# Two attention stages and a recurrence stage of a two-layer mixer: fetches on ScalarE's queue, queries and keys written reordered, a third PSUM bank

## The reference, cut to what matters

```
p = softmax(s)                                   # differential attention, 4 heads, two maps each
a = p[:, :, 0] - lam * p[:, :, 1]
y_a = rms_norm(a @ v) * ... * silu(az)

# mLSTM: chunkwise recurrence in both directions over 768 tokens, 4 heads of 128
num = a_inter * (q @ C) + (qk * exp(...)) @ v

# neighbourhood attention on a grid of 8 rows x 64 columns, 8 heads of 64
s_loc = q @ k[rows, 32 columns] * scale + bias   # for each block of 16 query columns
s_ctx = q @ k_ctx * scale
y_c = softmax([s_loc, s_ctx]) @ [v_loc, v_ctx] * silu(cz)

x = x + gate * (sum_n sigmoid(gm_n) * (y_n @ w_br_n)) @ w_out
```

## Time and profile before

| | |
|---|---|
| median of 3 runs | 3079.73 us |
| the profiled execution, its own time | 3081.52 us |
| span of its instructions | 3079.7 us |
| TensorE busy | 2865.6 us, 93% |
| VectorE busy | 1917.6 us, 62% |
| ScalarE busy | 1383.1 us, 45% |
| mean granted TensorE clock | 0.981 |

### The profile page before, as it was taken

One profiled execution on the slowest core, in us unless ns is written; L12 is line 12 of the kernel. 1 busy time (PEld: TensorE's weight loads), 2 busy tenths in 40 slices (PEclk: granted clock), 3 DMA queues, 4 the chain that ended last, 5 costly groups with the idle time before them and its releaser, 6 DMA issues. The chain is left out here.

```text
span 3079.7 us, 49691 instructions
## 1 busy us (share of the span) xinstructions
PE 2865.6 (93%) x19876; PEld 1760.7 (57%) x19876; DVE 1917.6 (62%) x3554; ACT 1383.1 (45%) x2817; POOL 35.7 (1%) x108
## 2 busy tenths in 40 slices
PE   7997899899999898899899989999999989999998
PEld 3564656755565464656544555366655656666654
DVE  6437666677534747766675568677734458777734
ACT  3236654454432336555454453444423248744422
POOL 0000000000000000000000000000000001100000
PEclk8999999999999999999999999999999989999999
DMA  8422321155432323331464323223324420023322
GB/s 334 170 79 63 76 94 62 56 149 118 88 113 79 104 81 88 83 100 69 145 155 139 113 81 117 89 83 112 108 95 134 134 74 2 21 91 110 110 94 84
DMA packets 190185, 315.56 MB, mean 102 GB/s; under 512 B 138589, under 2 KB 144349, under 8 KB 169349
## 3 DMA queue, kind: packets, MB, share of 16 engines
q1 hardware_dynamic: 185301, 307.01, 31.6%
q10 hardware_dynamic: 4656, 5.38, 0.5%
HBM read 261.83 MB, written 6.34 MB: 87 GB/s over the span
## 5 line engine op out<-in xcount | busy, mean ns | idle before, releaser
L315 PE MATMUL banks<-h_sb,wsplit_sb 128*128 128x512 f16 (+2 forms) x6528 | 1219.0, 340 | 64.8 <-PEq L86 19.6
L315 PEld LDWEIGHTS banks<-h_sb,wsplit_sb 128*128 128x128 f16 x6528 | 627.1, 99 | 567.4 <-issue 96.3
L315 PE MATMUL banks<-quads,wsplit_sb 128*128 128x512 f16 (+2 forms) x3300 | 589.9, 337 | 4.6 <-PEq L86 4.6
L290 ACT ACTIVATE wsplit_sb<-ring_sb 128x1024 f16<-128x1024 f32 (+2 forms) x356 | 330.1, 943 | 416.8 <-PE banks L315 374.6
L300 DVE SCALAR_TENSOR_TENSOR wsplit_sb<-ring_sb,wsplit_sb 128x1024 f16<-128x1024 f32 (+2 forms) x356 | 381.9, 1088 | 217.4 <-ACT wsplit_sb L290 215.4
L315 PEld LDWEIGHTS banks<-quads,wsplit_sb 128*128 128x128 f16 x3300 | 320.7, 98 | 256.4 <-issue 10.6
L315 PE MATMUL banks<-wsplit_sb,h_sb 128*128 128x256 f16 x2112 | 242.8, 274 | 7.9 <-ACT quads L559 3.2
L315 PEld LDWEIGHTS banks<-wsplit_sb,h_sb 128*128 128x128 f16 x2112 | 205.4, 98 | 41.3 <-issue 15.4
L2791 PE MATMUL banks<-h_sb,wsplit_sb 128*128 128x512 f16 x864 | 189.4, 379 | 0.0
L2791 PEld LDWEIGHTS banks<-h_sb,wsplit_sb 128*128 128x128 f16 x864 | 84.5, 98 | 98.1
L368 DVE SCALAR_TENSOR_TENSOR quads<-banks,quads 128x256 f16<-128x256 f32 (+1 forms) x80 | 49.9, 623 | 115.5 <-ACT quads L367 115.4
(11 more groups left out here) (407 smaller groups left out, 3641.4 us busy)
## 6 DMA issues: line engine op xcount, KB each, us to landing
ring_sb<-in_w_in SPq DMA_DIRECT2D x52, 1024.0 KB, 5.0
ring_sb<-in_w_ffn SPq DMA_DIRECT2D x44, 1024.0 KB, 4.7
ring_sb<-in_w_merge SPq DMA_DIRECT2D x48, 768.0 KB, 4.5
ring_sb<-in_w_ffn SPq DMA_DIRECT2D x32, 704.0 KB, 4.0
quads<-in_w_mod SPq DMA_DIRECT2D x12, 1024.0 KB, 23.7
x_sb<-in_w_mod SPq DMA_DIRECT2D x12, 1024.0 KB, 7.1
ring_sb<-in_w_ab SPq DMA_DIRECT2D x12, 1024.0 KB, 5.0
ring_sb<-in_w_nsa SPq DMA_DIRECT2D x10, 1024.0 KB, 5.5
```

Of the source, the lines that this page charges most:

```text
L290: act.activation(m.wsplit[:, s, 0, half * n:half * n + n], m.ring[:, s, half * n:half * n + n], ACT.Copy, scale=WSCALE).then_inc(w.hi[s], 1)
L315: mm = pe.matmul(p.bank, *p.terms(k, pw, px), start=(p.opens and k == 0 and z == 0), stop=(p.closes and k == p.depth - 1 and z == 2))
```

## The change

1. `firsts` goes. The second map is multiplied by -lambda * s0 / s1 and added to the unscaled first map; the rate of the first is applied where the high half is written (`highs`, with a scale) and where the low half is (`lows`, now a multiply and subtract). `rates` has one small instruction more. Some due times move.
2. In `diff_window` and `neighbour_window` `d.fetch` runs on ScalarE's stream and queue in place of SyncE's.
3. In `mlstm_window` the query and key parts of 512 tokens get `p.order`: TensorE's output goes to PSUM in the final order, from tokens read in their own order. The stores then read and write in one run (keys), or in blocks of 128 (queries). `query_low` goes.
4. In `mlstm_window` the parts from the queries on use three banks (4, 7, 6 in turn), bank 4 from when the norm is done.
5. In `mlstm_window` stores have due times 1.2 later (`late`), which puts them behind more of the recurrence's work in the streams.

```diff
@@ class Dense, __init__
+                place = banks[bank % len(banks)]
+                if third and i >= third[1]:
+                    place = ((banks + third[0:1])[::-1])[(i - third[1]) % 3]
+                p.after = held.get(place)
+                p.free = third[2] if third and place == third[0] and place not in held else None
@@ class Dense, product and stores
-            mm = pe.matmul(p.bank, *p.terms(k, pw, px), start=(p.opens and k == 0 and z == 0),
+            out, (lhsT, rhs) = p.bank, p.terms(k, pw, px)
+            if p.order:
+                out, rhs = p.order(out), by_token(p.order, rhs)
+            mm = pe.matmul(out, lhsT, rhs, start=(p.opens and k == 0 and z == 0),
...
-            yield p.t1 + (0.7 if p.high else 0.0)
+            yield p.t1 + self.late + (0.7 if p.high else 0.0)
@@ class Attention
-    def firsts(self, act):
-        for u, unit in enumerate(self.units):
-            yield self.when("first", u)
-            act.wait_ge(self.rated, u + 1)
-            act.activation(self.mixed(u), self.mixed(u), ACT.Copy, scale=self.rate(u)[:, 0:1]).then_inc(self.first, 1)
...
-            act.activation(self.W[:, 0:unit.nk], self.mixed(u), ACT.Copy).then_inc(self.high, 1)
+            act.activation(self.W[:, 0:unit.nk], self.mixed(u), ACT.Copy, scale=self.rate(u)[:, 0:1]).then_inc(self.high, 1)
...
-            dve.tensor_tensor(self.W[:, nk:2 * nk], self.mixed(u), self.W[:, 0:nk], ALU.subtract).then_inc(self.low, 1)
+            dve.scalar_tensor_tensor(self.W[:, nk:2 * nk], self.mixed(u), self.rate(u)[:, 0:1], self.W[:, 0:nk], ALU.mult,
+                                     ALU.subtract).then_inc(self.low, 1)
@@ diff_window
-        return dve.tensor_tensor(r, r, m.lam_rate[:, l, :], ALU.mult)
+        step(dve.scalar_tensor_tensor(r[:, 1:2], r[:, 1:2], m.neglam[:, l:l + 1], s[:, 0:1], ALU.mult, ALU.mult))
+        return dve.tensor_tensor(r[:, 0:1], r[:, 0:1], m.lam_rate[:, l:l + 1], ALU.mult)
...
-        a = Attention(m, units, asems, 0.0, d.span / (len(units) + 2.2), (0, .15, .35, .6, .65, .74, .85, .95, 1.1, 1.95, 2.15),
+        a = Attention(m, units, asems, 0.0, d.span / (len(units) + 2.2), (0, .15, .35, .6, .64, .76, .86, .98, 1.95, 2.15),
...
-            weave(gate_in(sp), d.fetch(sp), a.transposes(sp))
+            weave(gate_in(sp), a.transposes(sp))
...
-            weave(a.exps(act), a.firsts(act), a.highs(act), a.outs(act), gate_act(act), conv_act(act), d.split_hi(act), d.stores(act, "act"))
+            weave(a.exps(act), a.highs(act), a.outs(act), gate_act(act), conv_act(act), d.fetch(act), d.split_hi(act), d.stores(act, "act"))
@@ mlstm_window
-                    if p.n == S:
-                        p.high, p.store = split_store(order(out[0]), order(out[1]), lambda x, order=order: by_token(order, x))
-                        if first == 8:
-                            p.store = query_low(*out)
-                    else:
-                        p.high, p.store = split_store(out[0], out[1], by_query if first == 8 else lambda x: x)
+                    p.order = order if p.n == S else None
+                    p.high, p.store = split_store(out[0], out[1], by_query if first == 8 else lambda x: x)
...
-        d = Dense(m, wt, parts, (6, 7), dsems, extra=2.1 * len(units) + 6.0, high_done=high_done)
+        d = Dense(m, wt, parts, (6, 7), dsems, extra=2.1 * len(units) + 6.0, high_done=high_done, third=(4, 4 * len(qchunks), norm.done()),
+                  late=1.2)
@@ neighbour_window
-            weave(tables_in(sp), shifts(sp), d.fetch(sp), transposes(sp))
+            weave(tables_in(sp), shifts(sp), transposes(sp))
...
-            weave(norm.root(act), norm.highs(act), exps(act), highs(act), outs(act), d.split_hi(act), d.stores(act, "act"))
+            weave(norm.root(act), norm.highs(act), exps(act), highs(act), outs(act), d.fetch(act), d.split_hi(act), d.stores(act, "act"))
```

More of the change, by code:

```diff
@@ L211, in __init__ @@
         self.g, self.n, self.depth, self.terms, self.by, self.store = g, n, depth, terms, by, store
-        self.high = high
+        self.high, self.order = high, None
         self.before, self.hold, self.needs, self.ready, self.mate = before, hold, needs, ready, mate
@@ L219, with __init__ @@
 class Dense:
-    def __init__(self, m, weights, parts, banks, sems, extra=0.0, early=None, ahead=1, then=None, prior=None, high_done=None):
+    def __init__(self, m, weights, parts, banks, sems, extra=0.0, early=None, ahead=1, then=None, prior=None, high_done=None,
+                 third=None, late=0.0):
         self.m, self.weights, self.parts, self.banks = m, weights, parts, banks
-        self.high_done = high_done
+        self.high_done, self.late = high_done, late
         self.mm, out_act, out_dve = sems
@@ L237, in __init__ @@
                 bank += 1
-                p.after = held.get(bank % len(banks))
-            p.bank = m.ps[0:p.rows, banks[bank % len(banks)], 0:p.n]
+                place = banks[bank % len(banks)]
[3 more added lines that the diff above has]
+                p.free = third[2] if third and place == third[0] and place not in held else None
+            p.bank = m.ps[0:p.rows, place, 0:p.n]
             if p.closes:
@@ L242, in __init__ @@
                 p.nth = count[p.by]
-                held[bank % len(banks)] = p
+                held[place] = p
             self.upto[p.g], self.finish[p.g] = i + 1, p.t1
@@ L307, in open @@
             pe.wait_ge(*p.before)
+        if p.opens and p.free:
+            pe.wait_ge(*p.free)
         if p.opens and p.after:
@@ L356, in highs @@
             if p.high:
-                yield p.t1
+                yield p.t1 + self.late
                 act.wait_ge(self.mm, i + 1)
@@ L618, in __init__ @@
         self.m, self.units, self.at, self.t0, self.period = m, units, at, t0, period
-        (self.scored, self.pre_done, self.exp_done, self.rated, self.first, self.weighted, self.high, self.low, *self.turned,
+        (self.scored, self.pre_done, self.exp_done, self.rated, self.weighted, self.high, self.low, *self.turned,
          self.multiplied, self.out_copied, self.vsteps, self.squared) = sems
@@ L625, in __init__ @@
         self.o = m.ps[:, obank, 0:P]
-        self.names = {"scores": 0, "pre": 1, "mid": 2, "rates": 3, "first": 4, "post": 5, "high": 6, "low": 7, "trans": 8, "pv": 9, "out": 10}
+        self.names = {"scores": 0, "pre": 1, "mid": 2, "rates": 3, "post": 4, "high": 5, "low": 6, "trans": 7, "pv": 8, "out": 9}
     def when(self, name, u):
@@ L687, in after @@
             yield self.when("post", u)
-            dve.wait_ge(self.first, u + 1)
             self.post(dve, u, unit, self).then_inc(self.weighted, 1)
@@ L729, in outs @@
             act.activation(unit.dest, self.o[:, r0:r1], ACT.Copy, scale=self.unit_rate).then_inc(self.out_copied, 1)
-ATTENTION = ("scores", "pre", "exp", "rates", "first", "weights", "whi", "wlo", "tr0", "tr1", "pv", "out", "vsteps", "squared")
+ATTENTION = ("scores", "pre", "exp", "rates", "weights", "whi", "wlo", "tr0", "tr1", "pv", "out", "vsteps", "squared")
 DENSE = ("mm", "da", "dd")
@@ L940, in lambda_dve @@
             step(dve.tensor_scalar(m.lam_unit, m.lam_unit, 1.0, UNSCALE, ALU.add, ALU.mult))
-            step(dve.reciprocal(m.lam_rate[:, :, 0], m.lam_unit))
-            step(dve.tensor_tensor(m.lam_rate[:, :, 1], m.lam_rate[:, :, 0], m.neglam, ALU.mult))
+            step(dve.reciprocal(m.lam_rate, m.lam_unit))
         def rows(pe):
@@ L1266, in rates @@
         step(dve.reciprocal(r, s))
-        return dve.tensor_tensor(r, r, m.lam_rate[:, l, :], ALU.mult)
+        step(dve.scalar_tensor_tensor(r[:, 1:2], r[:, 1:2], m.neglam[:, l:l + 1], s[:, 0:1], ALU.mult, ALU.mult))
+        return dve.tensor_tensor(r[:, 0:1], r[:, 0:1], m.lam_rate[:, l:l + 1], ALU.mult)
     def post(dve, u, unit, a):
         nk, e = unit.nk, E[:, u % 2]
+        dve.wait_ge(a.rated, u + 1)
         return dve.scalar_tensor_tensor(e[:, 0:nk], e[:, nk:2 * nk], a.rate(u)[:, 1:2], e[:, 0:nk], ALU.mult, ALU.add)
@@ L1872, in value_half @@
     return rows.bitcast(F16)[:, z * BW:(z + 1) * BW]
-def query_low(high, low):
-    def store(dve, p):
-        for b in range(S // P):
-            out = dve.scalar_tensor_tensor(by_block(low)[:, :, b], by_token(by_block, p)[:, :, b], UNSCALE, by_block(high)[:, :, b],
-                                           ALU.mult, ALU.subtract)
-        return out
-    return store
 def by_column(x):
@@ L3656, in build @@
         m.lam_unit = sb("lam_unit", P, DEPTH)[:, :]
-        m.lam_rate = sb("lam_rate", P, DEPTH, 2)[:, :, :]
+        m.lam_rate = sb("lam_rate", P, DEPTH)[:, :]
         m.da_gain = sb("da_gain", P, DEPTH)
```

## The result

The changed kernel takes 3109.16 us (median of 4 runs, 3104.79 to 3110.92) against 3079.81 for the kernel before (four runs now): slower by 0.9%, ratio 1.0091 with a 95% interval of 1.0079 to 1.0102. The forecast was 3047, its range 3031 to 3090.

A forecast was written before the change was run, and what follows sets the result against it. TensorE, busy for 93% of the span, was taken as the bound, so only its waits could shrink. Terms -14.3 - 4 + 1.5 - 7.5 - 5 + 0 - 3 = -32.3 us took 3081.5 to 3049.2, as median 3047; range 3031 to 3090.

The forecast's parts named there:

- TensorE's own part of the stores' order: Recurrence stages, 192 key matmuls writing PSUM with a 32-byte step: taken as 0, half rate would be +41.5 us.
- The first rival: Recurrence stages: TensorE writes keys at half rate, +41.5 us, 3089 in all; decides from 0.39 us a matmul; chance 0.22.
- Fetches on another queue: Both attention stages: transposes no longer land late behind 1 MB fetches, -4 us (0 to 7.6); price +1.5.
- The price of ScalarE's stops: Attention stages: ScalarE's stream stops at each of 48 moved fetches until VectorE has split the last group, +1.5 us (0 to 6).
- SyncE's transposes there lose a wait ahead of them: Neighbourhood attention: moving fetches frees SyncE's transposes of a wait, but TensorE is idle for only 7.9 of 237 us.
- The scaling that goes: Differential attention: chain to the transpose 0.65 us shorter per unit, 22 waits, -14.3 us (bounds 7 and 17).
- Third bank: Recurrence stages: TensorE's waits for a bank VectorE has not yet stored all go, -7.5 us, lower bound 4.
- Stores in final order: Recurrence stages: key stores shorten to 0.6 and 0.7 us, cutting waits for VectorE's links, -5 us (0 to 10.9).
- Clock: Stages with much idle time: fewer waits keep TensorE's granted clock higher, -3 us (0 to 8).

The follow-up runs named there:

- the probe: Changed kernel with another access pattern for each of the eight key parts; only key matmul distances read: 216 or 429 ns for writes, 862 or 900 for strided reads.
- a_fetch_sp: Changed kernel with the weight fetches of both attention stages back on SyncE's queue: 3090.4 us, ratio 1.0036 to the kernel before.
- a_keys_plain: Changed kernel with key parts written by TensorE in token order again and reordered by the stores: 3079.6 us, ratio 1.0000 to the kernel before.
- a_keys_read: Changed kernel with keys reordered where TensorE reads the tokens, and written to PSUM without a step: 3211.3 us, ratio 1.0426 to the kernel before.

## Why the prediction was wrong, point by point

**TensorE's own part of the stores' order: the step that failed.** The sum took 0 for it, because "order alone isn't what costs" for runs of 16, and because the nearest rows were of other engines. Measured: 0.213 us for each of 192 matmuls, 40.9 us. The first rival had this size (41.5) and its cause; its condition, 0.39 us for a matmul, was passed (0.429). The queries' runs of 16 said nothing on single values, and the probe shows that even runs of 2 are free: the row that was taken as evidence lies on the other side of the step. With the rival's term alone the sum would have been 3089, still 20 short.

**Fetches on another queue: wrong sign.** Forecast -4 + 1.5. Undone in the changed kernel it is 18.8 us, alone on the kernel before 10.6. The gain of 4 supposed that a transpose waits for a fetch because of its queue; it is as late beside one of another queue (5.88 and 5.82 us). On the kernel before the gain was about 0 (A0 +0.9, A1 -0.2), the lower end of 0 to 7.6; in the changed kernel it was below that, as A0 fell by 4.8 when the move was undone. Its reading of the rows was off too: the seven transposes land 1.3 to 3.2 us later than the median of 3.6, not 2.2 to 3.1, and no row gives the 7.6. The price of ScalarE's stops was in its bounds (0 to 6), or a little over (7.9, at the edge of the noise). What no bound held: SyncE's stream, in order, had kept the fetches behind the transposes of a pair, and ScalarE's doesn't. "SyncE's transposes there lose a wait ahead of them" counted this as a gain.

**The scaling that goes: right.** -14.3 forecast, 13.5 by the ratio alone, 15.0 by the waits (39.5 to 24.5). The chain shrank by 0.55 instead of 0.65; the rest goes with what wasn't foreseen, that only 2 transposes are left close behind a fetch instead of 7 (argued, not tested by itself). In the changed kernel the fetches took back 9.9 us of it (a wait of 33.9, against 24.0 in a_fetch_sp).

**Third bank: the waits go as said, most of the time doesn't.** -7.5 forecast with a lower bound of 4; -3.2 measured. The waits for the bank went, and 5.2 us of them came back as waits for the next links of the recurrence's chain; with later due times and the queries' order R0 and R1 fell by 6.8 in a_keys_plain. These two were not run alone, and 6.8 is not far above what a stage's length wanders by.

**Stores in final order: too small.** -5 forecast with a bound of 10.9; 11.3 measured beside the third bank. Together with the third bank it was 12.5 forecast; the measured R stages less the 40.9 are 17.5 shorter, with the other parts in it.

**Clock.** No gain: the mean is 0.978 against 0.981, and in the untouched stage 0.93 against 0.97, which goes with 5 us more. Of why that stage differs nothing was tried; it varies between kernels that are the same there.

The parts make 40.9 - 11.3 - 13.5 + 18.8 - 6.8 = +28.1, where +29.4 was measured. They come from different kernels, so that they meet within 1.3 us is in part luck. Why the fetches cost 18.8 beside the shorter chain and 10.6 without is shown only by the counts of collisions; the intervals leave the split between stops and the rest open to some 5 us, and the rest holds the issuing on ScalarE besides the collisions.

## What to carry to other kernels

A reordering is to be put where a step is free. Here that was the PSUM read of ScalarE and VectorE; with a step of 16 bytes in the fp16 operands in SBUF ScalarE's store took 4.2 times as long (2460 against 589 ns) and VectorE's 3.5 times, TensorE's PSUM writes of single fp32 values twice (429 against 216 ns), and its strided reads four times (862 and 900). Swapping two loops of a store, one line, gave more (-9.9 us) than the third bank and cost nothing; look for it before moving the work to the engine that bounds the kernel. And before a DMA leaves a queue, see what the order in that queue kept apart: a transpose close behind a 1 MB fetch was 2.3 us late here, and one behind 768 KB about 1 us, whichever queue issued the fetch.

## What the hardware showed that was not expected

Matmuls of 512 columns whose moving tokens are read with a step took 862 ns (64 values apart) and 900 ns (8 apart), and as long at a granted clock of 1.00 as at 0.50: in the three windows of a_keys_read they start 861 to 863 ns apart throughout, and in the probe twelve took 10.96 us at a mean granted clock of 0.77 and twelve 10.99 at 0.50. TensorE was busy without a pause there, and still the granted clock went from 1.00 to 0.50, from the 2.4 to the 1.2 GHz level, while it ran them; that took the matmuls behind them along (256 columns in 213 ns instead of 109). Why it fell no run here shows. The strided writes did not bring it down: it is 1.00 in all eight strided key parts of the changed kernel. A PSUM read with a step of 256 bytes by ScalarE and VectorE took no longer than one run (589 and 689 ns).
